# The convolution branch's input tiles from the fifth on with a 512-column operand

## What is computed

```python
h = rms_norm(x, norm1_g[l])
z = h @ w_in[l]
u_pool, u_conf, u_sc, gate_logits = jnp.split(z, [OFF_POOL, OFF_CONF, OFF_SCONV], axis=-1)
br_a = multiscale_pool(u_pool, pool_w[l], pool_scale[l]) @ pool_proj[l]
val, gte = jnp.split(u_conf, 2, axis=-1)
v = val * jax.nn.sigmoid(gte)
v = causal_dwconv(v, conf_conv_w[l]) + conf_conv_b[l]
v = jax.nn.silu(layer_norm(v, conf_ln_g[l], conf_ln_b[l]))
br_b = v @ conf_proj[l]
```

## Time and profile before

| | |
|---|---|
| Median of 3 runs | 3222.53 us (3221.61 to 3223.65) |
| The profiled execution | 3222.01 us, of which its span is 3220.2 us |
| TensorE busy (matmuls) | 3183.9 us, 99% of the span |
| VectorE busy | 2347.3 us, 73% |
| ScalarE busy | 1438.4 us, 45% |
| GpSimd busy | 671.0 us, 21% |
| Granted TensorE clock | 0.999 in the mean |

### The profile page before, as it was taken

How to read it: one execution, slowest core, us unless ns; L and a number is a source line. 1 busy time by engine, 2 the same in 40 slices (tenths; PEclk the granted TensorE clock), 3 DMA queues, 4 the chain that set the end, 5 groups by cost and what they waited for, 6 DMA issues and landing times.

```text
span 3220.2 us, 54713 instructions
## 1 busy us (share of the span) xinstructions
PE 3183.9 (99%) x19498; PEld 2728.1 (85%) x19498; DVE 2347.3 (73%) x3449; ACT 1438.4 (45%) x2216; POOL 671.0 (21%) x590
## 2 busy tenths in 40 slices
PE   8999999999999999999999999999999999999999
PEld 8988988888998888889888787788878888888978
DVE  7888877667877677777776776667668776875765
ACT  5444446554444444444542433532352463453353
POOL 5999940111450000000300011000001100210000
PEclk9999999999999999999999999999999999999999
DMA  6555555565577777676633332134325543424435
GB/s 227 183 185 183 185 189 189 190 210 183 199 245 251 270 245 271 232 268 234 227 131 110 112 124 92 59 119 147 113 92 203 207 154 119 131 93 149 153 103 175
DMA packets 159869, 559.65 MB, mean 174 GB/s; under 512 B 17552, under 2 KB 23840, under 8 KB 159264
## 3 DMA queue, kind: packets, MB, share of 16 engines
q1 hardware_dynamic: 154144, 534.60, 48.7%
q0 software_dynamic: 5504, 22.04, 2.1%
HBM read 550.26 MB, written 6.31 MB: 173 GB/s over the span
## 4 chain that ended last, share of the span: by engine, by line
PE 72%; issue 19%; DVE 4%; ACT 1%; POOL 1%; POOLq 1%; DVEq 1%; DMA 0%; ACTq 0%; SPq 0%
PE psum L2281 14%; PE psum L2285 14%; PE psum L2282 14%; PE psum L2308 13%; PE psum L2309 6%; PE psum L2651 3%; PE psum L2677 2%; PE psum L2661 2%; DVE wlo L1413 1%; POOL thirdcat L2841 1%; PE psum L2464 1%; POOLq L2894 1%; PE psum L2465 0%; PE psum L2615 0%; DVEq L1399 0%
## 5 line engine op out<-in xcount | busy, mean ns | idle before, releaser
L908 ACT ACTIVATE whi<-raw 128x1024 fp32r<-128x1024 f32 (+3 forms) x844 | 862.6, 1029 | 914.3 <-DMA raw<-in_stream 383.4
L1413 DVE TENSOR_TENSOR wlo<-raw,whi 128x1024 fp32r<-128x1024 f32 (+3 forms) x844 | 1039.6, 1241 | 301.9 <-ACT whi L908 272.5
L2281 PE MATMUL psum<-hcat,whi 128*128 128x256 f32 (+1 forms) x2924 | 976.2, 334 | 3.5 <-DVE wlo L1413 2.8
L2285 PE MATMUL psum<-hcat,wlo 128*128 128x256 f32 (+1 forms) x2924 | 965.2, 330 | 0.8 <-DVE gate_half L1957 0.8
L2282 PE MATMUL psum<-hcat,whi 128*128 128x256 f32 (+1 forms) x2924 | 965.2, 330 | 0.0
L2308 PE MATMUL psum<-hcat,whi 128*128 128x512 f32 x2560 | 903.1, 397 | 1.5 <-POOL hcat L2841 0.9
L2309 PE MATMUL psum<-hcat,wlo 128*128 128x256 f32 x2560 | 717.8, 280 | 0.0
L2281 PEld LDWEIGHTS psum<-hcat,whi 128*128 128x128 f32 x2924 | 556.0, 190 | 64.0 <-issue 11.0
L2285 PEld LDWEIGHTS psum<-hcat,wlo 128*128 128x128 f32 x2924 | 555.8, 190 | 52.4 <-issue 1.2
L2282 PEld LDWEIGHTS psum<-hcat,whi 128*128 128x128 f32 x2924 | 556.1, 190 | 49.4 <-issue 0.5
L2308 PEld LDWEIGHTS psum<-hcat,whi 128*128 128x128 f32 x2560 | 480.3, 188 | 123.4 <-issue 9.2
(11 more groups left out here) (318 smaller groups left out, 3461.9 us busy)
## 6 DMA issues: line engine op xcount, KB each, us to landing
raw<-in_stream SPq DMA_DIRECT2D x978, 512.0 KB, 3.4
raw<-in_stream SPq DMA_DIRECT2D x18, 384.0 KB, 3.0
raw<-in_stream SPq DMA_DIRECT2D x24, 256.0 KB, 2.9
resid_dram<-X POOLq DMA_DIRECT2D x2, 2048.0 KB, 9.8
crow<-c_dram POOLq DMA_DIRECT2D x4, 1024.0 KB, 10.0
bias<-in_natten POOLq DMA_DIRECT2D x16, 256.0 KB, 2.9
X<-resid_dram POOLq DMA_DIRECT2D x4, 1024.0 KB, 6.2
raw<-in_stream SPq DMA_DIRECT2D x16, 192.0 KB, 2.5
```

Source lines behind the costliest of these rows:

```text
L908: act.activation(whi[:, c % HI_SLOTS, 0:n], raw[:, slot, 0:n], ACT.Copy).then_inc(hi_ready, 1)
L1413: vec.tensor_tensor(wlo[:, slot, 0:n], raw[:, slot, 0:n], whi[:, c % HI_SLOTS, 0:n].bitcast(F32), ALU.subtract).then_inc(lo_ready, 1)
L2281: pe.matmul(dst, h, cat[:, kk, c0:c0 + width], start=(q == 0 and k == 0), stop=False)
L2285: last = pe.matmul(dst, l_, cat[:, kk, c0:c0 + width], start=False, stop=(q == nq - 1 and k == nch - 1))
```

## The change

For the 12 tiles of the rolled loop TensorE calls `wide_tile` with stripe S instead of `tile`: two matmuls a chunk, over both halves of the bank. Tiles 0 to 3 stay as they are.

ScalarE, in odd k of the loop, after its rounding of normalized x: it waits for the tile's end and for `conf_added` (that the copy two tiles before has been read), and copies the bank's right half into the right half of `tmp`. VectorE, instead of waiting for the tile and multiplying out of PSUM: waits for that copy (`conf_right`), adds left half and copy into `half` (which frees the bank), drains, and multiplies `half` by `rst_of(norm1)` in place; after the gate tile it drains again and tells ScalarE, as before. Two semaphores are new.

```diff
@@ ScalarE, conf(i), odd k, after the rounding of normalized x
+                        if not isinstance(i, int):
+                            t = k // 2
+                            act.wait_ge(weights_used, Q0["conf"] + k + SLOTS + 8 * i + 1)
+                            act.wait_ge(conf_added, 4 * i + (t - 3))
+                            act.activation(tmp[:, t % 2, S:2 * S], psum[:, (T0["conf"] + t) % BANKS, S:2 * S],
+                                           ACT.Copy).then_inc(conf_right, 1)
@@ VectorE
             vec.sem_inc(psum_free, BANKS)
+            vec.sem_inc(conf_added, 2)
@@ VectorE, conf(i)
+                    elif not isinstance(i, int):
+                        t = k // 2
+                        part = half[:, 1 - t % 2, :]
+                        vec.wait_ge(conf_right, 4 * i + (t - 3))
+                        vec.tensor_tensor(part, ps, tmp[:, t % 2, S:2 * S], ALU.add).then_inc(psum_free, 1)
+                        vec.drain().then_inc(conf_added, 1)
+                        vec.tensor_tensor(part, part, rst_of(norm1), ALU.mult)
+                        if t % 2:
+                            vec.drain().then_inc(gate_scaled, 1)
                     elif k % 4 == 1:
                         tile_done(s, d)
                         vec.tensor_tensor(half[:, 1, :], ps, rst_of(norm1), ALU.mult).then_inc(psum_free, 1)
@@ TensorE
-            tiles("conf", 16, 4, hcat, S, 2 * S, S, skip=2)
+            for t in (2, 3):
+                tile(C0["conf"] + 2 * t, 0, T0["conf"] + t, 0, hcat, S, 2 * S, S)
+            with pe.Fori(1, 4) as i_:
+                for t in range(4):
+                    wide_tile(C0["conf"] + 2 * t, 8 * i_, T0["conf"] + t, 4 * i_, S)
```

## The result

| | before | after |
|---|---|---|
| Median | 3222.58 us (7 runs) | 3233.59 us (7 runs, 3230.85 to 3236.6) |
| Ratio | | 1.0035, interval 1.0025 to 1.0044 |
| Profiled execution | 3222.01 us, span 3220.2 | 3233.59 us, span 3231.8 |
| VectorE busy | 2347.3 us | 2353.3 us |
| GpSimd busy | 671.0 us | 680.3 us |

A forecast was written before the change was run, and what follows sets the result against it. The prediction took TensorE's matmul stream to bound the kernel: 3222.01 us less 1.23 from wide chunks, every other cost covered by slack, gave 3220.8, or 3221.3 us as median. The range was 3218.5 to 3225.5 us.

The forecast's parts named there:

- What bounds the kernel: Changed stage: TensorE's matmul stream bounds it; time is saved only by fewer matmul-microseconds or fewer TensorE stalls.
- The gain, 1.23 us: Rolled loop's twelve tiles: a wide chunk takes 0.3533 us instead of 0.360, over 184 chunks 1.23 us less.
- VectorE's account: Changed stage: with 0.55 and 0.03 us added per tile, VectorE works 10.97 us per pair of tiles, against 11.3 available.
- Nearly full but does not accumulate: VectorE in the changed stage: 0.3 us spare per pair, so the long half's 0.5 us lateness is taken back.
- the waits forecast for its short half: VectorE's waits for TensorE at the tile's end become waits for ScalarE's copy, in the short half only.
- GpSimd's taps are self-paced; they end before its 6.00 us wait: Taps end before GpSimd's wait for the branch's last taps from VectorE; TensorE 1.2 us earlier leaves 4.8.
- The gain passes the pool stage: VectorE's 31 us chain to TensorE's matmul at 170.60 comes 1.2 us earlier; 3.0 us of waits cover lateness.
- The rivals: Gain lost on the way, 3222.5 us (0.18); pool chain shorter by chance, 3219.8 (0.09); VectorE overfull, 3224 to 3226 (0.10).
- the slower one: Changed stage: VectorE overfull because of GpSimd, SBUF products at 0.87 us, TensorE stalls 2.3 us; 3224 to 3226 us, chance 0.10.
- The sum: Whole kernel: profiled execution 3222.01 less 1.23 gives 3220.8 us; 0.52 more for the median, 3221.3 us.

The follow-up runs named there:

- wide_only: Changed kernel without ScalarE's copy and VectorE's addition; the wide matmuls' right half is dropped in the twelve tiles: 3224.47 us, ratio 1.0001.
- before_six_taps: Kernel before, with GpSimd doing six taps instead of seven between two low parts of the short convolution stage: 3222.68 us, ratio 0.9995.
- six_taps: Changed kernel, with GpSimd doing six taps instead of seven between two low parts of the short convolution stage: 3229.9 us, ratio 1.0021.
- sum_in_psum: Changed kernel, but VectorE writes the sum back to PSUM and the multiplication by rst reads it there: 3234.26 us, ratio 1.0034.
- extra_psum: Kernel before plus one more VectorE multiplication per tile out of PSUM, behind a drain, its result unread: 3229.32 us, ratio 1.0019.
- after_again: The changed kernel, unchanged, run a second time beside other runs: 3236.82 us, ratio 1.0037.
- after_padded: Changed kernel with 128 increments of an unused semaphore at the head of TensorE's program: 3251.5 us, ratio 1.0086.

## Why the prediction was wrong

**What bounds the kernel**: right, and not enough. That TensorE bounds the stage says nothing of who is one step from bounding it later. The earlier trace rows showed GpSimd busy 43.02 of 46.00 us, and I read on to VectorE.

**The gain, 1.23 us**: right, and it came. In after two wide chunks, 33 apart, start 11.66 us apart, 0.3533 us, as in the earlier trace rows, and 175 chunks take 1.17 us less than in before:

```profile
69.78 0.40 PE L2326 MATMUL psum<-hcat,whi 128*128 128x512 f32 x1
...
81.44 0.40 PE L2326 MATMUL psum<-hcat,whi 128*128 128x512 f32 x1
```

The lead at 124 us is a bad measure of it. After is 2.2 us ahead there, wide_only 0.95; but before_six_taps, which has no wide tile there, is 1.86 ahead as well. In before the first tile of the loop takes 7.35 us, at a granted clock of 0.53 from 39 to 42 us; in after 5.76, at 1.00, and in before_six_taps 5.85, at 1.00, though TensorE had waited longer ahead of it in both (2.27 and 2.14 us against 1.76). Whether the clock falls there differs between executions, and that alone is 1.5 us, more than the gain. What decides it no run shows.

**VectorE's account**: the terms were right or too high. The addition takes 0.412 us and the product out of SBUF 0.426, from 60 to 111 us:

```profile
L1571 DVE TENSOR_TENSOR half<-half,rst 128x256 f32<-128x256 f32 x9 | 3.8, 426 | 1.2
L1569 DVE TENSOR_TENSOR half<-psum,tmp 128x256 f32<-128x256 f32 x9 | 3.7, 412 | 0.0
```

TensorE doesn't wait inside the stage. A pair took VectorE 11.0 us (five pairs, from the addition at 52.15 us to that at 107.14), where 10.97 was forecast. "Nearly full but does not accumulate" is what happened, for VectorE. One thing was otherwise: it waited for none of the twelve copies. It came into the loop late, 1.6 us behind the start of the first copy, and was 0.4 behind that of the last, so the waits forecast for its short half were not there.

**"GpSimd's taps are self-paced; they end before its 6.00 us wait"**: this is the step that failed, twice over. Self-paced was read as unaffected, though a tap that starts within the large subtract takes twice as long. And the wait at 437.99 us was taken for GpSimd's only appointment; the one at 296 us, where VectorE waits 1.49 us for it and TensorE's weights stand behind, was in the same trace and wasn't looked for. Six microseconds of lateness there cost 9.7, where the step gave zero. The wait at 437.99 us did have room: in six_taps, whose taps are late, GpSimd still waits 1.75 us there. I had asked who waits for VectorE, not who waits for GpSimd.

**The gain passes the pool stage**: right without the additions: TensorE's matmul of 170.60 starts at 169.6 in wide_only, 1.0 us earlier. In after it starts at 168.3, but of the lead of 2.2 us 0.87 is left by the 297 us conversion, and six_taps has lost all of its own there. No run shows what took it.

**The rivals**: the slower one had the right engine pair and the wrong effect. It expected twelve products of 0.87 us and VectorE late inside the stage; the products stayed at 0.43, and the price was paid by GpSimd, 180 us later. Its 3226 us lacked the stall's size, and the code load altogether. The rule of the Trainium skill (SBUF — State Buffer, "Who interferes with whom"), cited there for the new multiplications, fits the old subtracts: sum_in_psum and extra_psum show that the new instructions' operands don't matter to the total.

**The sum**: 3220.8 was forecast for the profiled execution, 3233.59 came. The step on GpSimd was short by 9.7 us; the code load gave 1.9, the last stages 1.9; some 1.2 us came back between 352 and 2226 us. Of the last stages' part only the `csq` wait, 0.3 us, goes with the change, and in other executions what the clock adds; the pace is chance.

**A version that beats both**: none was found. six_taps less its code load would stand near before (my estimate, from its being level with before at 352 us); wide_only shows 0.7 to 1.0 us of gain in its trace and none in its median; before_six_taps is level with before.

## What to carry to other kernels

An engine's idle time may be what another engine runs in, and it matters where the gaps lie, not only how long they are. Before giving VectorE work beside a busy GpSimd, look for the first place where anybody waits for GpSimd, however far behind the change, and read the slack there: a wait that is already there, as the 1.49 us at 296 us, means none. And a change of program length moves the code loads; after a small edit, look at whether a load that somebody waits for has got one beside it. A gain of a microsecond is read from equal stretches of the stream, not from the total.

## What the runs showed of the hardware

Twelve added PSUM products on VectorE, 0.43 us each, raised the mean of GpSimd's taps from 1192 to 1491 ns; taps that start within VectorE's large subtract take 2.1 us, those beside its waits or PSUM products 0.9 (before, after, extra_psum). A 16 KB code packet that started 1.6 to 1.7 us behind the issue of a 1 MB load took 1.4 to 1.8 us of one DMA engine and lengthened VectorE's wait for the load by 2 to 3 us (after, sum_in_psum, six_taps, after_again). With 128 semaphore increments at the head of TensorE's program the first weight load, which waits for a signal behind them, is issued 18.8 us later, an estimate of 0.15 us each (after_padded). One kernel's last stage runs at one of two paces, 2.78 or 2.83 us per 128 x 1024 quarter, at the same granted clock of 1.00 (after_again, after).
